# The second down projection's weight sums: accumulating DMAs between places in DRAM, issued by GpSimd, in place of VectorE's additions

## What is computed

```python
for l in range(DEPTH):                      # second_block, DEPTH = 1
    z = rms_norm(h, attn_norm[l]) @ w_in[l]
    ...
    h = h + jnp.concatenate([o_nsa, o_gla], axis=-1) @ w_out[l]
    u = causal_dwconv(rms_norm(h, ffn_norm[l]) @ w_up[l], conv_w[l], conv_b[l])
    gate, up = jnp.split(u, 2, axis=-1)
    h = h + (jax.nn.silu(gate) * up) @ w_down[l]
```

## Time and profile before

| | us |
|---|---|
| three executions, lowest / median / highest | 1521.63 / 1522.67 / 1524.0 |
| the profiled execution, first to last instruction (span) | 1520.9 |
| PE busy in it | 1499.2 |
| DVE busy | 1026.8 |
| ACT busy | 661.2 |
| POOL busy | 46.2 |

### The profile page before, as it was taken

The page is one execution under the profiler, slowest core; times in us unless marked ns, Lnnn a source line. Parts: engine busy times, 40 slices in busy tenths (PEclk is TensorE's granted clock), DMA queues, the critical chain, the costliest instruction groups (busy, mean ns, idle before and its releaser), DMA issues.

```text
span 1520.9 us, 21091 instructions
## 1 busy us (share of the span) xinstructions
PE 1499.2 (99%) x8527; PEld 1224.3 (80%) x8527; DVE 1026.8 (68%) x1773; ACT 661.2 (43%) x1090; POOL 46.2 (3%) x82
## 2 busy tenths in 40 slices
PE   7999999999999999999999999999999999999999
PEld 5777888778888898888888777777788988888887
DVE  6679886766588666444459876787567456556885
ACT  4453334653222342222246553766525434434653
POOL 0000000000000000000000021200011000000000
PEclk9999999999999999999999999999999999999999
DMA  9423122149778457665535515100113232232473
GB/s 385 146 83 97 56 70 84 57 181 343 271 267 307 153 187 285 233 222 200 201 127 184 180 60 222 56 30 29 57 56 129 93 107 85 86 111 97 135 229 128
DMA packets 77210, 229.29 MB, mean 151 GB/s; under 512 B 6453, under 2 KB 6581, under 8 KB 75961
## 3 DMA queue, kind: packets, MB, share of 16 engines
q1 hardware_dynamic: 77112, 227.94, 42.9%
HBM read 202.75 MB, written 25.17 MB: 150 GB/s over the span
## 4 chain that ended last, share of the span: by engine, by line
PE 91%; DVE 5%; ACT 3%; issue 1%; POOL 0%; DMA 0%; SPq 0%; DVEq 0%; ACTq 0%
PE bank L696 86%; PE bank L708 4%; DVE AR L1922 1%; DVE wl L1900 1%; ACT wh L1376 0%; DVE G L1929 0%; DVE AR L2232 0%; DVE X L1922 0%; DVE Hl L1922 0%; DVE X L1929 0%; ACT AR L1387 0%; DVE ST L1922 0%; DMA CST<-in_cst 0%; ACT AR L1399 0%; ACT AR L1774 0%
## 5 line engine op out<-in xcount | busy, mean ns | idle before, releaser
L1376 ACT ACTIVATE wh<-raw 128x1024 fp32r<-128x1024 f32 (+1 forms) x223 | 230.6, 1035 | 363.2 <-PE bank L696 317.7
L1900 DVE TENSOR_TENSOR wl<-raw,wh 128x1024 fp32r<-128x1024 f32 (+1 forms) x223 | 263.7, 1192 | 91.7 <-ACT wh L1376 91.6
L696 PE MATMUL bank<-wh,Hh 128*128 128x512 f32 (+1 forms) x726 | 293.1, 404 | 3.8 <-DVE wl L1900 2.5
L696 PE MATMUL bank<-wh,Hl 128*128 128x512 f32 (+1 forms) x726 | 281.1, 387 | 0.0
L696 PE MATMUL bank<-wl,Hh 128*128 128x512 f32 (+1 forms) x726 | 280.3, 386 | 0.0
L696 PE MATMUL bank<-Hh,wh 128*128 128x512 f32 (+2 forms) x712 | 268.5, 377 | 0.2
L696 PE MATMUL bank<-Hl,wh 128*128 128x512 f32 (+2 forms) x712 | 266.9, 375 | 0.0
L696 PE MATMUL bank<-Hh,wl 128*128 128x512 f32 (+2 forms) x712 | 266.9, 375 | 0.0
L696 PEld LDWEIGHTS bank<-wh,Hh 128*128 128x128 f32 x726 | 136.5, 188 | 38.6 <-issue 9.7
L696 PEld LDWEIGHTS bank<-wh,Hl 128*128 128x128 f32 x726 | 136.3, 188 | 28.5
L696 PEld LDWEIGHTS bank<-wl,Hh 128*128 128x128 f32 x726 | 136.8, 188 | 23.4
(11 more groups left out here) (271 smaller groups left out, 2022.2 us busy)
## 6 DMA issues: line engine op xcount, KB each, us to landing
raw<-in_wst SPq DMA_DIRECT2D x224, 512.0 KB, 4.2
CST<-in_down SPq DMA_DIRECT2D x22, 1024.0 KB, 5.9
sums_dram<-CST SPq DMA_DIRECT2D x22, 1024.0 KB, 4.8
raw<-sums_dram SPq DMA_DIRECT2D x40, 512.0 KB, 3.9
raw<-in_down SPq DMA_DIRECT2D x30, 512.0 KB, 3.6
AR<-in_wst SPq DMA_DIRECT2D x8, 1024.0 KB, 11.3
X<-in_x SPq DMA_DIRECT2D x8, 512.0 KB, 6.0
AR<-in_wst SPq DMA_DIRECT2D x5, 512.0 KB, 5.3
```

The source lines that it names most:

```text
L696: return e.matmul(o, l, r, start=start, stop=stop, skip_group_check=True)
L1376: e.activation(HI[slot[i]][:, 0:width(i)], raw[:, i % NR, 0:width(i)], ACT.Copy).then_inc(*w_hi.mark(i))
L1900: e.tensor_tensor(LO[slot[i]][:, 0:n], raw[:, i % NR, 0:n], HI[slot[i]][:, 0:n].bitcast(f32), SUB).then_inc(*w_lo.mark(i))
```

## The change

The first block's sums stay as they are. For the second block the loads into `SUMT`, the four additions and the stores are gone from the up stage. In their place POOL issues 11 DMAs from DRAM to DRAM, each of a whole quarter (11 x 128 rows of 2 KB, 2.88 MB). Four are copies, which start the four sums; seven add their source to what the destination holds (`accum_op=ADD`): four second terms, two third terms, one fourth term. A term may only be added once the one before it has landed, so POOL waits for semaphore counts (`s_halves`, `s_kept`) before it goes on. The down stage's loads by SP wait for `s_kept` to reach 112, the count of all seven additions.

Since a DMA can only add, the sums are redefined without differences: the signs move to the left sides (`left_sum`) and to the places where the products are added up. For "6" a left sum becomes `scalar_tensor_tensor` with -1.0, in both blocks.

```diff
-    todo = [(key, p) for key in SEVEN for p in range(11)]
-    early = [k for k, t in enumerate(ticks) if t[0] in EARLY]
-    late = [k for k, t in enumerate(ticks) if t[0] == "up" and t[1][0] > 0]
-    for among, every, after in ((early, 12, 6), (late, 10 / 3, 2)):
...
+    among = [k for k, t in enumerate(ticks) if t[0] in EARLY]
+    for p in range(11):
+        load[among[12 * p]].append(("dn", p))
+        add[among[12 * p + 6]].append(("dn", p))
+        store[among[12 * p + 6]].append(("dn", p))
...
-            return s_sums, 16 * (11 * SEVEN.index(key) + p + 1)
+            return (s_sums, 16 * (p + 1)) if key == "dn" else (s_kept, 112)
...
-                tt(b22, b22, b12, SUB)
+                tt(b22, b22, b12, ADD)
                 own()
-                tt(b12, b12, b11, SUB)
+                tt(b12, b12, b11, ADD)
                 tt(b11, b11, b22, ADD)
                 own()
-                tt(b21, b21, b11, SUB, ("right sums", key, p))
+                tt(b21, b21, b11, ADD, ("right sums", key, p))
...
-                a, b = {"6": (group("4", u), group("7", u)), "5": (group("1", u), group("6", u)), "3": (group("2", u), group("6", u))}[z]
-                tt(group(z, u), a, b, ADD if z == "5" else SUB, (key, "left sum", z, u))
+                if z == "6":
+                    stt(group(z, u), group("7", u), -1.0, group("4", u), MUL, SUB, (key, "left sum", z, u))
+                else:
+                    tt(group(z, u), group({"5": "1", "3": "2"}[z], u), group("6", u), ADD, (key, "left sum", z, u))
...
         def pool_program(e, on):
+            quarters = down_in[1].rearrange("(a q p) (h c) -> q h a p c", q=2, p=P, h=2)
+            kept = {z: sums_dram[1, i] for i, z in enumerate(SUMMED)}
+
+            def copies():
+                for z, q in (("7", (1, 1)), ("5", (0, 1)), ("6", (0, 1)), ("4", (0, 1))):
+                    e.dma_start(kept[z], quarters[q]).then_inc(s_halves, 16)
+
+            def second_terms():
+                on.wait_ge(s_halves, 64)
+                for z, q in (("7", (0, 1)), ("5", (0, 0)), ("6", (0, 0)), ("4", (0, 0))):
+                    e.dma_start(kept[z], quarters[q], accum_op=ADD).then_inc(s_kept, 16)
+
+            def third_terms():
+                on.wait_ge(s_kept, 64)
+                for z in "64":
+                    e.dma_start(kept[z], quarters[1, 1], accum_op=ADD).then_inc(s_kept, 16)
+
+            def fourth_term():
+                on.wait_ge(s_kept, 96)
+                e.dma_start(kept["4"], quarters[1, 0], accum_op=ADD).then_inc(s_kept, 16)
...
             for name in ("ks", "kw"):
                 root(ST[:, 48:56], dve.of((name, "sum")), (name, "root"))
+            copies()
             for t in range(T):
                 if t == 2:
                     root(ST[0:64, 60:61], dve.of(("csum",)), ("croot",))
                 root(ST[:, 592 + 8 * t:600 + 8 * t], dve.of(("nq", "sum", t)), ("nq", "root", t))
+            second_terms()
+            third_terms()
+            fourth_term()
             for t in range(T):
                 root(ST[:, 48:52], dve.of(("lsum", t)), ("lroot", t))
```

More of the change, by code:

```diff
@@ L418, in program @@
         s_cst, s_cst2, s_prm, s_bc, s_out = (sem(n) for n in ("s_cst", "s_cst2", "s_prm", "s_bc", "s_out"))
-        s_pair, s_sums = sem("s_pair"), sem("s_sums")
+        s_pair, s_sums, s_halves, s_kept = (sem(n) for n in ("s_pair", "s_sums", "s_halves", "s_kept"))
         s_in = [sem(f"s_in{t}") for t in range(T)]
@@ L605, in stored @@
         def stored(key, p):
-            return s_sums, 16 * (11 * SEVEN.index(key) + p + 1)
+            return (s_sums, 16 * (p + 1)) if key == "dn" else (s_kept, 112)
         def pair_in(key, p):
-            return s_pair, 16 * (11 * SEVEN.index(key) + p + 1)
+            return s_pair, 16 * (p + 1)
         def group(z, u):
@@ L2443, in added @@
                 on.wait_ge(*dense.of(("dn", z, r)))
-                tt(to, a, bank[BANKS[z][r]][:, :], ADD, ("dn", event, r))
+                b = bank[BANKS[z][r]][:, :]
+                if z in "53":
+                    tt(to, b, a, SUB, ("dn", event, r))
+                else:
+                    tt(to, a, b, ADD, ("dn", event, r))
             for s, z, g, rows in w.steps("dn"):
@@ L2457, in vector_program @@
                         on.wait_ge(*act.of(("dn", "u", r)))
-                        tt(SGR[2 + r], SGR[2 + r], SGR[r], ADD)
+                        tt(SGR[2 + r], SGR[2 + r], SGR[r], SUB)
                         gated(SGR[2 + r], 1, 2 + r)
@@ L2794, in add_product @@
                 xs = X[:, 2 * h + r, 512 * n:512 * n + 512]
-                tt(xs, xs, bank[BANKS[z][r]][:, :], ADD, ("2dn", event, r))
+                tt(xs, xs, bank[BANKS[z][r]][:, :], SUB if z in "76" and n == 1 else ADD, ("2dn", event, r))
             ADDED_AT = {14: ("7", "c22 7", 1, 1), 16: ("1", "c11 1", 0, 0), 20: ("2", "c11", 0, 0), 26: ("5", "c22 5", 1, 1),
```

## The result

| | before | after |
|---|---|---|
| median of four executions, us | 1522.24 | 1555.33 |
| lowest to highest | 1521.63 to 1524.0 | 1554.13 to 1556.56 |
| span of the profiled execution | 1520.9 | 1553.4 |
| ratio of after to before, 95% interval | | 1.0217 [1.0204, 1.0229] |

The change costs 33.1 us. The time lies within the range given, and its direction is the one forecast, but it came about by another case than the one held likeliest, which stood at 1526.9 us.

The account below looks back on a forecast made before the run. PE, busy 1499.2 of 1520.9 us, was taken as the bound; the terms 0 + 0 + 4.2 + 0 gave +4.2 us, added to the median of 1522.67 for 1526.9 us, range 1520.5 to 1570.

Parts of the forecast that it names:

- the one held likeliest: Copies' issues delay root "nq" 0, additions finish before root "lroot" 0: 1526.9 us, own range 1523 to 1540, chance 0.40.
- What is removed: Up stage: 44 additions on DVE and 22 transfers of 1 MB go, PE never waits there: 0 us.
- Changed signs: Left sums and product additions: swapped additions and subtractions, and scalar_tensor_tensor for "6", cost what they did: 0 us.
- The four copies' issues: POOL ahead of root "nq" 0: 5.5 us an issue, 22 for four, delaying PE's transpose: +4.2 us; decides from 4.45.
- The chain of additions: POOL's waits before "lroot" 0: 170 ns a packet, free at 1101.0, 14 us to spare: 0; decides from 193 ns.
- The chain of additions runs into lroot 0: Rival: at 255 ns a packet POOL reaches "lroot" 0 40.2 us late, +44 us in all, 1567 us; chance 0.20.
- SP's loads: Rival: SP's weight loads slow beside the new packets, over 20 us a load: +5 to +20 us, 1535; chance 0.05.
- Faster: Rival: up stage without DVE's additions and 22 MB gives 13 ns on some 860 matmuls, 11 us, 1511.5; chance 0.06.
- "nq" 0 at 952: Sign that the prediction is wrong: this root was to move from 952.1 to near 963.6 us.
- a wait of POOL ahead of "lroot" 0: Sign that the prediction is wrong: "lroot" 0, expected about 1114.5 with DVE as releaser, released by a DMA's semaphore.
- nearer 7.8 us: Sign in the up stages: DVE's busy time of 20 us falls there, with PE again at 90 matmuls.

Follow-up runs that it names:

- Experiment 3: The changed kernel without its 11 DMAs, the last product reading the first block's sums, so the second block's sums are left out: 1522.14 us, ratio 1.0000.
- experiment 2: The changed kernel with the same transfers and waits, each DMA naming its 128 rows as outermost dimension instead of the 11 blocks: 1522.62 us, ratio 1.0002.
- experiments 1: The changed kernel with the fourth term's wait and DMA moved behind the four roots "n4": 1522.47 us, ratio to before 1.0001.

## Why the prediction was right in its range and wrong in its likeliest case

In short: the direction and the range came out right, and in part by luck. The forecast took its +4.2 us from the copies' issues, which cost nothing. The loss came from the chain of additions, which stood in the sum at 0. The range reached up to 1570 for additions of 255 ns a packet, which did not come; what came in their place was a held issue, which it did not have.

- **What is removed: 0.** Right. Experiment 3 gives 1.0000, and the up stage keeps its 90 matmuls in 20 us.
- **Changed signs: 0.** Right, by the same run.
- **The four copies' issues, +4.2 us.** The step that failed. The size taken, 5.5 us an issue as the work of 11 blocks of rows, was five times too large: four take 4.52 us, so one takes 1.1, under the 4.45 from which it decides, and the term is 0. What the prediction set beside it from the Trainium skill ("DMA: Bandwidth & Descriptors", section "Anatomy of one DMA — SWDGE (gpsimd) path"), that descriptor generation is a small part, agrees with this row.
- **The chain of additions, 0.** This step failed too, and it is the one that cost 33 us. Its arithmetic foresaw the mechanism and missed the size. POOL was to be free at 1101.0 and was at 1141.4. The 40.4 us are made up as follows: the copies held the start until 991.3 and not 983.7, +7.6 (they took 50 us and not 30; over all 16 engines, in experiment 2, they still took 45.6, 941.60 to 987.18, so the uneven spread is the smaller part, and a copy beside the loads is slower than the 85 ns a packet that were taken from a store); the second terms issued together took 71.6 us (991.32 to 1062.95) where 66.8 was said for all four, +4.8; the held fourth took 28.4 alone (1062.95 to 1091.38); the third terms took 48.1, not 45.0, +3.1; the last issue 2.0, not 5.5, -3.5. So 28.4 of 40.4 us are a thing that the prediction did not know, the held issue. The packet, 186 ns against 170 taken, stayed below the 193 from which it called the term decided (its own sum, 123.0 / 640, gives 192).
- **Without the hold?** Three additions on 11 engines each already put 3 x 128 pieces on one engine, and a fourth fits beside them, so at 186 ns the chain would have ended near 991.3 + 71.6 + 48.1 + 1.9 = 1112.9, some 2 us late. This is worked out, not run.
- **The rivals.** "The chain of additions runs into lroot 0" is what happened: 1567 said, 1555.3 measured, the difference being that it put 255 ns a packet where the runs showed 186 and a hold, and 4.2 us for the first term. SP's loads did get slower, with a median of 7.0 us for 17 of them between 935 and 1160 against 3.5, and its buffers covered that, as experiments 1 and 2 show. "Faster" had nothing behind it.
- **What the profile was to show.** "nq" 0 at 952, and a wait of POOL ahead of "lroot" 0 that a DMA ends: both marks of a wrong likeliest case are there. The low clock behind the wait, 2.7 us, was not in the sum. For DVE in the up stage it said "nearer 7.8 us" of 20, and 6.1 were measured; its own rows give 9.3 - 29.4 x 20 / 195 = 6.3.

## What to carry to other kernels

A wait for a transfer's completion on an engine that works in order is an appointment for everything behind it: put each dependent step of such a chain behind the engine's next urgent piece of work, not ahead of it (one call moved behind eight roots gave all 33 us back). Count the engines that a transfer's outermost dimension can be spread over: 11 for 16 made each addition half as long again. And before removing work from an engine, ask what would be faster if it took no time at all; here a version with none of it answered "nothing".

## What the runs showed of the hardware that I had not expected

- GpSimd can be held in the issue of a transfer with no semaphore of the program behind it: 65.8 us for one addition of 2.75 MiB while three were outstanding. The held issue goes when all that is outstanding has landed. The room goes by an amount: 3.5 additions over 11 engines (3.5 x 128 = 448 rows) or 5 over 16 (5 x 88 = 440 rows for each engine) passed, and 512 and 528 did not. A plain copy took half of that (7 passed, the 8th was held). This counts all 16 engines alike, with 128 for an addition over 11, also those that have no data. That is an inference, but the packets fit it: such an addition leaves 2064 packets, one over 16 engines 1424, and the 640 more are 5 x 128. How transfers that have landed still count stays open.
- An addition from DRAM to DRAM takes 186 ns for each 2 KB on an engine, against 85 ns for the same packet of a plain store; alone, 2.75 MiB take 18.9 us over 16 engines.
- Four copies of 2.75 MiB from DRAM to DRAM, issued by ScalarE, kept its queue for 30 us; issued by GpSimd they kept it for 4.5.
- After 30.5 us of idle PE restarts at the lower clock (0.50 granted): the first eight matmuls took 2.04 us in place of 1.05, and the restart cost 2.7 us in all. They took 2.04 also behind the 12.5 us wait of the kernel with second terms in halves.
